# Adding each fetched row in two halves of 512 columns in the last stage of a transformer-layer kernel

## The reference

```
act = gelu(einsum('td,thkd->thk', h, u[expert]))
y   = einsum('thkd,thk->td', v[expert], gate * act)
x   = x + gate2 * y
```

## Time and the profile before

| | us |
|---|---|
| median of 3 runs | 3629.02 |
| lowest and highest | 3623.06, 3631.27 |
| time of the profiled execution | 3625.86 |
| its span | 3624.1 |
| first and last fetch of a row (L1997) start | 2789.4, 3584.7 |
| last addition of a row ends, about | 3602 |
| last matmul of the last chunk ends, about | 3609 |

### The profile page before, as it was taken

The page is one execution under the profiler, slowest core; times in us unless marked ns, Lnnn a source line. Parts: engine busy times, 40 slices in busy tenths (PEclk is TensorE's granted clock), DMA queues, the critical chain, the costliest instruction groups (busy, mean ns, idle before and its releaser), DMA issues. The chain is left out here.

```text
span 3624.1 us, 47830 instructions
## 1 busy us (share of the span) xinstructions
PE 3279.6 (90%) x18306; PEld 2875.8 (79%) x18306; DVE 2471.8 (68%) x4437; ACT 1414.7 (39%) x2526; POOL 1350.5 (37%) x1028
## 2 busy tenths in 40 slices
PE   5899999799589899699999999999996989888888
PEld 2677777688478789699999999999995767676777
DVE  5134344378643478688878878888885777677778
ACT  3134344277521321146655555556541222222222
POOL 0000000000000000034656566555556888888884
PEclk8999999899789999899999999999998999999999
DMA  7411210111133311268999899999999999999997
GB/s 282 156 62 45 74 59 30 51 47 56 64 129 113 128 36 48 89 227 294 359 365 365 325 383 392 329 362 376 329 334 340 362 324 320 317 328 318 327 314 289
DMA packets 314883, 828.71 MB, mean 229 GB/s; under 512 B 35104, under 2 KB 115360, under 8 KB 309152
## 3 DMA queue, kind: packets, MB, share of 16 engines
q1 hardware_dynamic: 195872, 422.82, 32.9%
q0 software_dynamic: 118784, 402.85, 30.3%
HBM read 712.82 MB, written 112.72 MB: 228 GB/s over the span
## 5 line engine op out<-in xcount | busy, mean ns | idle before, releaser
L1643 POOL DMA_INDIRECT s_row<-in_u_rows,back_expert x256 | 352.4, 1377 | 1818.6 <-DVE back_expert L1816 1555.5
L84 PE MATMUL s_ps_a<-back_dense_hi,s_u_hi 128*128 128x384 f32 x2048 | 701.1, 342 | 39.3 <-DVE s_u_lo L1706 39.3
L86 PE MATMUL s_ps_a<-back_dense_hi,s_u_lo 128*128 128x384 f32 x2048 | 690.3, 337 | 0.0
L85 PE MATMUL s_ps_a<-back_dense_lo,s_u_hi 128*128 128x384 f32 x2048 | 689.7, 337 | 0.0
L84 PE MATMUL c_ps_y<-back_dense_hi 128*128 128x512 f32 x1024 | 416.5, 407 | 114.6 <-DVE back_dense_lo L2063 83.9
L2038 DVE SCALAR_TENSOR_TENSOR c_y<-c_row,c_w,c_y 128x1024 f32<-128x1024 f32 x256 | 328.5, 1283 | 192.6 <-DMA c_row<-in_v,back_expert 179.3
L1643 POOL DMA_INDIRECT s_row<-in_v,back_expert x256 | 335.9, 1312 | 249.1 <-DVE back_y L1840 195.4
L84 PEld LDWEIGHTS s_ps_a<-back_dense_hi,s_u_hi 128*128 128x128 f32 x2048 | 389.3, 190 | 40.1 <-issue 34.1
L85 PE MATMUL c_ps_y<-back_dense_lo,back_dense_hi 128*128 128x512 f32 x1024 | 411.0, 401 | 0.0
L86 PE MATMUL c_ps_y<-back_dense_hi,back_dense_lo 128*128 128x512 f32 x1024 | 410.0, 400 | 0.0
L85 PEld LDWEIGHTS s_ps_a<-back_dense_lo,s_u_hi 128*128 128x128 f32 x2048 | 389.1, 190 | 0.0
(11 more groups left out here) (331 smaller groups left out, 6496.5 us busy)
## 6 DMA issues: line engine op xcount, KB each, us to landing
s_u_raw<-in_u SPq DMA_DIRECT2D x128, 512.0 KB
c_v_raw<-in_v SPq DMA_DIRECT2D x128, 512.0 KB
act_scratch<-s_a SPq DMA_DIRECT2D x128, 384.0 KB
gm_scratch<-s_gm SPq DMA_DIRECT2D x16, 2048.0 KB
c_a<-act_scratch SPq DMA_DIRECT2D x128, 256.0 KB
c_g<-gm_scratch SPq DMA_DIRECT2D x32, 1024.0 KB
a_w<-in_w_ada SPq DMA_DIRECT2D x24, 1024.0 KB, 7.8
gate_scratch<-at_gate SPq DMA_DIRECT2D x32, 256.0 KB, 2.0
```

The source lines that it names most:

```text
L84: nc.tensor.matmul(out, w_hi, x_hi, start=first, stop=False)
L85: nc.tensor.matmul(out, w_hi, x_lo, start=False, stop=False)
L86: return nc.tensor.matmul(out, w_lo, x_hi, start=False, stop=last)
L1643: gp.indirect_dma_start(out=row[:, n % R], out_offset=None, in_=table, in_offset=bass.IndirectOffsetOnAxis(ap=keep.expert[:, g, k:k + 1], ...
```

## The change

Each unit's operation of 1024 columns becomes two, of columns 0 to 511 and 512 to 1023. Both read the same row buffer and the same weight, and both count on the semaphore `used`, so every wait on `used` now asks for twice the count.

```diff
@@ fetch(n), GpSimd
                 if n >= R:
-                    gp.wait_ge(used, n - R + 1)
+                    gp.wait_ge(used, 2 * (n - R + 1))
@@ unit(n), VectorE
                 else:
-                    dve.wait_ge(used, n - LOOKED + 1)
-                nc.vector.scalar_tensor_tensor(out=y[:, t], in0=row[:, n % R], scalar=w[:, t, k:k + 1], in1=y[:, t],
-                                               op0=ALU.mult, op1=ALU.add).then_inc(used, 1)
+                    dve.wait_ge(used, 2 * (n - LOOKED + 1))
+                for cols in (slice(0, HALF), slice(HALF, D)):
+                    nc.vector.scalar_tensor_tensor(out=y[:, t, cols], in0=row[:, n % R, cols], scalar=w[:, t, k:k + 1], in1=y[:, t, cols],
+                                                   op0=ALU.mult, op1=ALU.add).then_inc(used, 1)
@@ TensorE, ahead of the transposes
-            pe.wait_ge(used, UNITS)
+            pe.wait_ge(used, 2 * UNITS)
```

## The result

The changed kernel takes 3597.36 us in the median of 4 runs (3575.50 to 3607.31), against 3630.14 for the kernel before in 4 runs of its own. The ratio is 0.991, with a 95% interval of 0.988 to 0.994. A second measurement gave 3598.32 against 3620.07, ratio 0.992 (0.990 to 0.995). That is faster by 22 to 33 us, and both medians lie within the range forecast (3562 to 3616); its middle was 38 us and 3588. The profiled execution is the slowest of its four, 3607.31 with a span of 3605.5, so its rows show less of the gain than the median.

A forecast was written before the change was run, and what follows sets the result against it. GpSimd's issue of indirect DMAs was taken as the bound: 3625.86 less 38 us of holds, with VectorE's 36 us covered at 0, gave 3588 us. The forecast's own range was 3562 to 3616, the wider one 3555 to 3630.

The forecast's parts named there:

- The bound: Last stage, up to the last 16 fetches: GpSimd's issue of indirect DMAs sets the pace, one row in 3.20 us.
- The rival of the transfers: Rival: row transfers are the limit, so rows come no faster, 3626 us; chance half of the 0.10 for no change.
- The hold and its rule: GpSimd issues starting inside a two-SBUF-input VectorE instruction stand until it ends, finishing 0.81 or 0.82 us later; 175 us in all.
- VectorE's price: Row additions on VectorE: halves add 0.14 us a unit, 36 us over 256, covered by 179.3 us of waits for rows.
- The middle of a row is a door: Held issues get in between halves; rival that they do not: 3646 us, chance 0.12 shared with VectorE uncovered.
- The gain of 38 us: GpSimd's issues over 241 rows: shorter holds with halves take 0.16 us off each row, 38 us.
- both ways: Two estimates of GpSimd's gain: counting 162 issues in row additions, 39 us; assuming starts at any phase, 38 us.
- The locking dissolves: Rival: nearly all 79.5 us that issues stand in row additions go, down to 3546 us; chance 0.12.

The follow-up runs named there:

- the sum over a row: Kernel before with each row's weighted addition replaced by a one-input sum over its columns, the gathered part left out: 3553.74 us.
- 384 and 640: Changed kernel with each row cut into pieces of 384 and then 640 columns instead of halves: 3635.14 us.

## Why the prediction was right, point by point

- **The bound** (issues of indirect DMAs, not transfers) holds: without look-ups the kernel takes 3507 us, and the stretch adds up from issues, gaps and holds alone. The rival of the transfers falls: with the sum over a row all transfers are there and 74.5 us of the stretch are gone.
- **The hold and its rule** hold, and its condition is reading two inputs from SBUF, as far as the instructions here can tell it. The Trainium skill's page "SBUF — State Buffer", section "Who interferes with whom", says that VectorE instructions with two SBUF inputs contend with GpSimd instructions that read SBUF, and these holds agree. Its report that a tensor_tensor did not stall DMAs issued by GpSimd does not hold for the indirect ones here: L2057, a tensor_tensor, held 96 of them for 47 us. The measurement decides. The prediction stretched that report to the row addition, which is another operation.
- **VectorE's price** of 34 to 36 us, covered: 748 ns a half, and in the kernels without look-ups no cost clear of the spread is seen (5 us between medians), with next to no wait for rows to hide it in.
- **The middle of a row is a door**: of 94 issues that start in a first half 43 end 0.82 after it, 51 pass free, and none misses it. That rival falls as it was put.
- **The gain of 38 us** is the term that was mis-sized: the medians give 33 and 22, and the holds of 480 issues fell by 26 and 18. The row period came to 3.10 and 3.13 us, where 3.04 was forecast. It is also in another place than the count put it. The rows were to hold 39 us less, with the issues staying where they were. They hold 17 us more: 34.7 us up to the end of the own piece, and 61.0 with missed ends. The whole gain, and more, is in L2057 and L2063, 71.2 us before and 19.8 after, since the successors of released issues no longer land in them. The failed step is that both ways took the starts as given or as even, where each released issue sets the start of the next. The same sum gives 35 us for a cut at 640 (0.31 for the row in place of 0.29), where 25 are lost. So that the cut at 512 gained, and by near the forecast amount, was partly luck.
- **"The locking dissolves"** was a rival with 80 us. It does not; it takes on another pattern, and missed ends went from 17.0 to 88.7 us.

## What to carry to other kernels

Where GpSimd issues indirect DMAs without rest, look at their durations beside VectorE's timeline: an issue that starts in a VectorE instruction with two SBUF inputs waits for its end. What helped most here was to issue fewer DMAs (118 us in the kernel that leaves the look-ups out); a VectorE instruction that reads one input and writes one column held none (one that reads one input and writes a full row was not tried). Cutting instructions helps or hurts by where the next issue lands, so several cuts are measured, and the one with the best time (here rows and v_lo both in halves, 0.988) is kept. A count over a recorded timeline that leaves all other starts in place is not a forecast in such a loop.

## What was not expected of the hardware

- An issue takes 0.94 us, or ends 0.82 us after a VectorE instruction that held it, to within 0.01 us in 303 of 307 holds of the kernel before. By sums of 1.22 us with one input, and by a zeroing of 1.76 us with none, it is never held.
- An end of an instruction with the next one right behind can be missed, and the issue stands through one to three more: up to 2.77 us in the changed kernel, 3.41 with 384 and 640. Why is open.
- Moving a cut by 128 columns moves the whole kernel by 1.6%, 52 us (3597.36 and 3649.87).
- TensorE had stretches at 15 matmuls in 20 us with no releaser in the trace, in some kernels only. That stays open.
